# Second block of a two-block layer: scaled queries ahead of the diagonal's mask, the stick mixer's VectorE part a turn later, mixed tiles copied during the last gate tile

## The reference

```python
h = x @ w_in
o_nsa = nsa_mixer(...)             # three attention branches, 6 heads
o_sb = stick_breaking_mixer(...)   # 4 heads, blocks of 128 queries
o_hg = hgrn2_mixer(...)            # 6 heads, gated linear recurrence
o_hg = o_hg * rsqrt(mean(o_hg ** 2) + eps) * hg_norm_w
mixed = concatenate([o_nsa * silu(nsa_z), o_sb * silu(sb_z), o_hg * silu(hg_z)])
x = layer_norm(ALPHA * x + mixed @ w_out, ln_g, ln_b)

# stick breaking, for one block of queries
z = (q @ k.T) * scale
log_rest = where(mask, log_sigmoid(-z), 0)
between = reverse cumulative sum of log_rest, shifted by one
a = where(mask, exp(log_sigmoid(z) + between), 0)
o = a @ v
```

## Time and profile before

| | us |
| --- | --- |
| median of 3 runs | 1101.42 |
| lowest, highest | 1100.38, 1101.49 |
| the profiled execution, its own time | 1101.64 |
| span of that execution | 1099.4 |
| TensorE busy in the span | 1063.4 (97%) |
| VectorE, ScalarE, GpSimd busy | 619.1, 451.4, 27.4 |
| mean granted TensorE clock | 0.994 |

### The profile page before, as it was taken

How to read it: one execution, slowest core, us unless ns; L and a number is a source line. 1 busy time by engine, 2 the same in 40 slices (tenths; PEclk the granted TensorE clock), 3 DMA queues, 4 the chain that set the end, 5 groups by cost and what they waited for, 6 DMA issues and landing times.

```text
span 1099.4 us, 13928 instructions
## 1 busy us (share of the span) xinstructions
PE 1063.4 (97%) x5454; PEld 850.1 (77%) x5454; DVE 619.1 (56%) x1167; ACT 451.4 (41%) x825; POOL 27.4 (2%) x41
## 2 busy tenths in 40 slices
PE   6999999999999999999999999999998899999997
PEld 5877778888879888888888888988776686666575
DVE  5457654445355666532666634445685673566657
ACT  5344333232254444421343434543345456556640
POOL 0000000000011000000000000200000001000000
PEclk9999999999999999999999999999999999999999
DMA  7421123323332832341332233242111123310011
GB/s 264 154 78 58 58 77 96 96 96 96 118 115 74 298 106 89 118 129 55 96 96 96 96 124 125 92 144 80 57 56 49 39 87 98 151 56 27 16 58 77
DMA packets 29103, 107.06 MB, mean 97 GB/s; under 512 B 3226, under 2 KB 3370, under 8 KB 28400
## 3 DMA queue, kind: packets, MB, share of 16 engines
q1 hardware_dynamic: 24288, 84.04, 23.3%
q0 software_dynamic: 4032, 19.96, 5.2%
q10 hardware_dynamic: 720, 2.20, 0.5%
HBM read 101.44 MB, written 7.36 MB: 99 GB/s over the span
## 4 chain that ended last, share of the span: by engine, by line
PE 88%; DVE 6%; ACT 3%; issue 2%; DMA 1%; ACTq 0%; DVEq 0%; SPq 0%
PE ps L671 25%; PE ps L673 24%; PE ps L672 24%; PE ps L1050 2%; PE ps L1084 1%; PE ps L1067 1%; PE ps L945 1%; PE ps L811 1%; DVE wlo L1482 1%; PE ps L784 1%; PE ps L1017 1%; PE ps L796 1%; ACT whi L1149 1%; DMA XT<-xt 1%; PE ps L982 1%
## 5 line engine op out<-in xcount | busy, mean ns | idle before, releaser
L671 PE MATMUL ps<-XH,whi 128*128 128x512 f32 (+1 forms) x864 | 338.8, 392 | 9.9 <-DVE wlo L1499 8.3
L673 PE MATMUL ps<-XH,wlo 128*128 128x512 f32 (+1 forms) x864 | 328.2, 380 | 0.0
L672 PE MATMUL ps<-XL,whi 128*128 128x512 f32 (+1 forms) x864 | 328.0, 380 | 0.0
L1482 DVE TENSOR_TENSOR wlo<-raw,whi 128x1024 fp32r<-128x1024 f32 (+1 forms) x158 | 189.3, 1204 | 182.1 <-ACT whi L1149 182.0
L671 PEld LDWEIGHTS ps<-XH,whi 128*128 128x128 f32 x864 | 163.6, 189 | 50.7 <-issue 18.3
L1149 ACT CAST whi<-raw 128x1024 fp32r<-128x1024 f32 (+1 forms) x158 | 161.2, 1026 | 85.9 <-PE ps L673 57.5
L673 PEld LDWEIGHTS ps<-XH,wlo 128*128 128x128 f32 x864 | 163.4, 189 | 31.4
L672 PEld LDWEIGHTS ps<-XL,whi 128*128 128x128 f32 x864 | 163.8, 190 | 27.7 <-issue 0.5
L671 PE MATMUL ps<-whi,GH 128*128 128x512 f32 x176 | 68.9, 391 | 0.0
L672 PE MATMUL ps<-wlo,GH 128*128 128x512 f32 x176 | 68.6, 389 | 0.0
L673 PE MATMUL ps<-whi,GL 128*128 128x512 f32 x176 | 68.5, 389 | 0.0
(11 more groups left out here) (275 smaller groups left out, 1346.6 us busy)
## 6 DMA issues: line engine op xcount, KB each, us to landing
raw<-wp SPq DMA_DIRECT2D x150, 512.0 KB, 3.5
vec_dram<-row_dram POOLq DMA_DIRECT2D x1, 3072.0 KB, 13.1
H<-x POOLq DMA_DIRECT2D x1, 2048.0 KB, 8.1
x_dram<-H POOLq DMA_DIRECT2D x1, 2048.0 KB, 7.6
A<-w1c POOLq DMA_DIRECT2D x2, 1024.0 KB, 6.6
A<-x_dram POOLq DMA_DIRECT2D x1, 2048.0 KB, 12.7
y<-A SPq DMA_DIRECT2D x8, 256.0 KB, 2.0
raw<-wp SPq DMA_DIRECT2D x4, 402.0 KB, 3.6
```

The costliest lines, as they stand in the source:

```text
L671: self.e.matmul(o, ah, bh, start=start, stop=False)
L672: self.e.matmul(o, ah, bl, start=False, stop=False)
L673: return self.e.matmul(o, al, bh, start=False, stop=stop)
L1482: self.e.tensor_tensor(wlo[BUF[i]][:, 0:w], raw[i % NR][:, 0:w], whi[BUF[i]][:, 0:w].bitcast(F), ALU.subtract).then_inc(sems["lo"], 1)
```

## The change

Nothing is computed otherwise. In `hgrn()` the call of `h_q1` stands ahead of `h_diag`, and `h_prep(p, 0)` stands a turn later, behind `h_off(p, 0)`. In `stick()` VectorE's part of `s_first` becomes a stage of its own, `s_soft`, one turn later, and the diagonal's mask of `s_second` becomes `s_mask`, which runs at the head of the next block's `s_first` (after the last block, a turn later). TensorE's and ScalarE's parts stay in `s_first` and `s_second`. In `gates()` the first three `mix_tile` run in the turns of the last gate tile; a new semaphore `zx` says that this tile's matmuls have read the slices of XH that the copies overwrite; `out2` begins a turn earlier. ScalarE's load of the Exp table moves from behind its copy of the last stick result to ahead of it. `nsk` is merged into `vev`, whose waits count one higher.

```diff
@@ hgrn, stick @@
             en.h_start(p)
             yield
+            en.h_q1(p)
             en.h_diag(p)
-            en.h_q1(p)
-            en.h_prep(p, 0)
             yield
             en.h_off(p, 0)
+            en.h_prep(p, 0)
             en.h_prep(p, 1)
             en.h_mult(p, 0)
...
             for n in range(4):
+                if n:
+                    en.s_mask(p, n - 1)
                 en.s_first(p, n)
                 yield
+                en.s_soft(p, n)
                 yield
                 en.s_second(p, n)
                 yield
+            en.s_mask(p, 3)
             yield
             en.s_pv(p)
@@ gates @@
                 if n >= 4 and part == 1:
                     en.mix_mul(n - 4)
+                if n == 7 and part > 0:
+                    en.mix_tile(part - 1)
                 yield
         en.mix_mul(4)
-        en.mix_tile(0)
-        en.mix_tile(1)
+        en.mix_tile(3)
         yield
-        en.mix_tile(2)
+        en.out2(0, 0, 0)
+        en.mix_tile(4)
         yield
...
@@ Tensor @@
-                self.tile(B2_Z + n, part, 4, 2)
+                f = self.tile(B2_Z + n, part, 4, 2)
+                if n == 7 and part < 3:
+                    f.then_inc(sems["zx"], 1)
@@ Scalar @@
-            def nsa_begin(self):
-                self.e.preload_act_table_set(EXP)
...
             def s_pv(self, p):
+                if p == 1:
+                    self.e.preload_act_table_set(EXP)
                 self.wait_ge("s_av", p + 1)
...
                     self.wait_ge("t_m", n + 1)
-                    self.wait_ge("used", SLOT_WOUT2)
+                    if n // 2 < 3:
+                        self.wait_ge("zx", n // 2 + 1)
+                    else:
+                        self.wait_ge("used", SLOT_WOUT2)
@@ Vector @@
-            def s_first(self, p, n):
+            def s_soft(self, p, n):
...
+
+            def s_mask(self, p, n):
+                kb, at = 3 - n, 4 * p + n
                 for j in range(2):
                     diag = AA[j][kb][:, 0:128]
```

More of the change, by code:

```diff
@@ L83 @@
 sq eps rt rs pg nlo nhi tr xh xl tm res
-qev vev nsk qk tt ex t1 cp av sk skx nrm ft ahi alo
+qev vev qk tt ex t1 cp av sk skx nrm ft ahi alo
 cvc cvp cvy cvt cvz cvh cvl gt bra bm ma mh ml
 vem dm ve lb lbe ua ub sl um gh gl
-fb fc hk sc one kl0 qz hq hv hgt avv src nk nq sq2 sk2 zc zt
+fb fc hk sc one kl0 qz hq hv hgt avv src nk nq sq2 sk2 zc zt zx
 h_d h_x h_e h_dg h_ta h_qk h_k2 h_of h_oc h_p h_pe h_m h_pr h_av h_sq h_rm h_ln h_rs h_ot blk1
@@ L174 @@
     c_move = c_blk = c_mm = c_end = begin_norm = block2_after = idle
-    n_qk = n_scale = n_tr = n_pv = n_out = nsa_begin = s_first = s_second = s_pv = mix_mul = mix_tile = mix_rows = last = out2 = end = idle
+    n_qk = n_scale = n_tr = n_pv = n_out = nsa_begin = s_first = s_soft = s_second = s_mask = s_pv = mix_mul = mix_tile = mix_rows = last = out2 = end = idle
 class Engine(Stages):
@@ L444, in gates @@
                     en.mix_mul(n - 4)
+                if n == 7 and part > 0:
+                    en.mix_tile(part - 1)
                 yield
         en.mix_mul(4)
-        en.mix_tile(0)
-        en.mix_tile(1)
+        en.mix_tile(3)
         yield
-        en.mix_tile(2)
+        en.out2(0, 0, 0)
+        en.mix_tile(4)
         yield
[L452 to L459, removed]
+        en.out2(0, 0, 1)
+        en.mix_tile(5)
+        yield
+        en.out2(0, 1, 0)
+        en.mix_rows(0)
+        yield
+        en.out2(0, 1, 1)
+        en.mix_rows(1)
+        yield
         en.mix_rows(2)
@@ L780, in qk @@
                     self.wait_ge("qev", 5)
-                    self.wait_ge("vev", 1)
+                    self.wait_ge("vev", 2)
                     self.wait_ge("tt", 2 * n + j - 1)
@@ L791, in tr @@
                 self.wait_ge("cp", n)
-                self.wait_ge("vev", 2)
+                self.wait_ge("vev", 3)
                 self.wait_ge("par", 32)
@@ L805, in pv @@
                 self.wait_ge("cp", n + 1)
-                self.wait_ge("vev", 4)
+                self.wait_ge("vev", 5)
                 self.wait_ge("nrm", qb)
@@ L1572, in v @@
                     self.wait_ge("rs", 2)
-                    self.e.tensor_scalar(nsink, RW[:, R_SINK:R_SINK + 8], -1.0, None, ALU.mult).then_inc(sems["nsk"], 1)
+                    self.e.tensor_scalar(nsink, RW[:, R_SINK:R_SINK + 8], -1.0, None, ALU.mult).then_inc(sems["vev"], 1)
                 self.wait_ge(*rows_done(0, t, SLOT_V))
@@ L1583, in soft @@
                     self.wait_ge("qk", 2 * n + j + 1)
-                    self.wait_ge("nsk", 1)
+                    self.wait_ge("vev", 1)
                     self.wait_ge("av", n - 2)
```

1 line of the change is left out of this document (added).

## The result

| | before | after |
| --- | --- | --- |
| median, us | 1101.38 | 1108.82 |
| lowest to highest, four runs each | 1100.38 to 1101.49 | 1107.79 to 1109.06 |
| the profiled execution, its own time | 1101.64 | 1108.73 |
| its span, mean granted clock | 1099.4, 0.994 | 1106.5, 0.991 |

The changed kernel takes 1.0077 times as long as the one before (95% interval 1.0064 to 1.0089): 7.4 us more. 1108.2 was predicted, in a range of 1102.3 to 1113.5.

The account below looks back on a forecast made before the run. TensorE, busy for 97% of the span, was taken as the bound outside a few places. Terms -4.8 + 4.9 + 5.5 + 4.4 - 1.2 - 2.2 = +6.6 over 1101.64 gave 1108.2 us, range 1102.3 to 1113.5.

Parts of the forecast that it names:

- stick (0, 2), clock: Two waits below 2 us replace one of 2.53, so the clock stays up: -3.1 us, bounds 0 and -3.1.
- `h_prod` before (0, 3): Next level's h_prep and h_mult come ahead of VectorE's stick part, so h_prod's 2.17 us wait goes: -2.2.
- stick (1, 1), wait and clock: VectorE's part stands behind c_blk(1, 0), which awaits GpSimd's transfer: +4.9 us wait, +2.2 for the lower clock.
- stick (1, 3), wait and clock: VectorE's part stands behind the weight slot's low part, cast after Gelu's table loads: +5.5 us wait, +2.2 clock.
- nsa's begin: ScalarE's table load goes ahead of TensorE's last stick result into idle time; the 1.18 us wait goes: -1.2.
- tail, waits and clock: Gates' tail: the 1.81 us wait goes (-1.8), its low clock (-1.7), new waits +1.3; together -2.2.
- rival 1: The clock also falls at stick (0, 1) or (0, 2): +3.1, 1111.3 us; chance 0.22.
- The clock behind the two long waits: Lower clock after the waits at stick (1, 1) and (1, 3): 2.2 us each, +4.4; bounds 0 and 6.2.
- One sign of being wrong: The prediction is wrong if TensorE's low stretches are as many as before.
- The second: Rival: the clock stays up through the two long waits, as through 2.17: -4.4, 1103.8 us; chance 0.10.
- the fourth: Rival: neither long wait comes, only the gains: -14.8, 1093.4 us; chance 0.08.
- rival 3: Transfer before c_blk(1, 0) lands in 2.2 us, not 5.6; not slower: -5.6, 1102.6 us; chance 0.10.

Follow-up runs that it names:

- the second of the two transfer runs: Changed kernel with the small transfers, still behind the weight's wait for c_mm, issued ahead of the 1 MB transfer: 1102.80 us.
- the tail's run: Kernel before with the gates' tail and the Exp table load alone changed: 1097.52 us, ratio 0.9970.
- the fastest: Changed kernel with only VectorE's part of stick (0, 3) a turn later, other parts at once, masks right behind the second part: 1088.60 us.

## Why the prediction was right

| step | predicted | after shows |
| --- | --- | --- |
| two waits at `h_off` | -2.4 | -2.4 |
| stick (0, 1) | +1.8 | +1.63 |
| stick (0, 2), wait | -0.8 | -1.07 (2.53 to 1.46) |
| stick (0, 2), clock | -3.1 | -1.4 (3.06 to 1.65) |
| `h_prod` before (0, 3) | -2.2 | -2.17, and +0.5 at the picks |
| first `s_pv` | +1.9 | +1.62 |
| stick (1, 1), wait and clock | +4.9, +2.2 | +4.62, +3.0 |
| stick (1, 3), wait and clock | +5.5, +2.2 | +5.54, +1.64 |
| nsa's begin | -1.2 | -1.18 |
| tail, waits and clock | -0.5, -1.7 | -0.6, -1.7 |
| start of the kernel | none | -1.0 in this execution |
| sum | +6.6 | +7.0 (profiled executions: +7.09) |

The first line of the tail's prediction is its -1.8 and +1.3 together. The waits in the tail, from 960 us on, are after 1.5 + 0.8 + 0.3 + 0.2 = 2.8, before 2.5 + 0.5 + 0.4 = 3.4.

**The waits were right**, each within 0.3 us, since each came from the same question: what does the moved instruction now stand behind, and when is that released? Two runs confirm that the releaser was the right one. With (1, 1) at once -8.0 was measured, where the prediction's terms give -7.1; with (1, 3) at once -8.3, against -7.7. The parts that were to gain did so as well: -6.6 for the queries (-8.0 was expected of that run), -3.7 for the tail with nsa's begin (the terms give -3.4).

**The step that was off is the clock at stick (0, 2).** I took it that the clock stays up because two shorter waits stand in place of one of 2.53, and gave the other case to rival 1. What happened lies in between: the clock fell behind a wait of 1.46, but for some 3.4 us instead of 6.8. The reason I gave, the length of the wait, doesn't decide it. Six other runs have the same two waits of 1.6 and 1.4 to 1.5 here. In one of them (with (1, 1) at once) the clock fell, in five it stayed up, as in this one (the second pair at once):

```profile
848.75 0.91 PE L1031 MATMUL ps<-A,C 128*128 128x384 f32 x2 [1.45 <-DVE A L1929]
```

The first two matmuls take 0.91 us here, at the full clock, and 1.47 in the changed kernel's profile. So this term is a chance and not a value, and -3.1 was the end of its range, not its middle.

The clock behind the two long waits was the same kind of guess at 2.2 each, and measured 3.0 and 1.64. It differs since both low stretches are 6.8 us long, but at (1, 1) TensorE stands idle in 0.8 of it and at (1, 3) in 3.5. These two misses cancel within 0.3.

**The sum is in part luck.** All clock terms together were put at -0.4 (-3.1, +4.4, -1.7) and came to +1.5. That the sum is only 0.4 off is due to the start of the kernel, -1.0 in this execution, and to the waits, which were a little shorter than predicted; without the start the rows give +8.0. The start is chance: the first block is the same in all kernels here, and its wait of 1.25 ended between 30.0 and 32.0 us over their profiles. The medians moved by +7.4.

**One sign of being wrong doesn't fit the forecast.** It says that low stretches as many as before would refute it. Before there were two, and the forecast itself puts two in their place, behind stick (1, 1) and (1, 3). There were three; the one near 850 is what the forecast didn't have, and it is in part rival 1.

**A term that was missing** is the one for the picks. With `h_prod` no longer late, TensorE comes earlier to the next one and waits for its pick (0.97 instead of 0.46): +0.5.

**The rivals.** The second (clock up through the long waits) and the fourth (no long waits) fell with the trace. The third, the early landing, needed the transfer to land within 3.2 us. After the change it was issued at 883.54, VectorE was idle from 885.03 on for 4.29 us, and it landed in 5.7 us, not 2.2. The Trainium skill, SBUF - State Buffer, section SBUF: two separate sides, has GpSimd unable to write its descriptors while VectorE runs an operation on both ports, so that an idle VectorE would let the transfer land early. The two landings go the other way: it was late with VectorE idle for most of it, and early, in the second of the two transfer runs, with VectorE at work for most of it. Whether VectorE's operations there use both ports, no run shows. What shortened the landing, at an issue time 0.5 us apart, was to move the 1 MB transfer from ahead of it to behind it. The Trainium skill, DMA: Bandwidth & Descriptors, section Two DMAs through the same engine are not ordered, says that descriptors start in order within one queue of one DMA engine, and with that the two runs agree. The price of rival 3 was sound, though not its cause: with the landing at 2.2 us the kernel takes 1102.8, where it gave 1102.6.

## What to carry to other kernels

In queues that run in order, a step that is moved to give its engine more slack also takes over the waits of everything it is moved behind: list for each instance what now stands ahead and when that is released. One order for all instances of a loop was the mistake here: of eight blocks two lost some 8 us each by the later turn, two others 3.8 together, and one, (0, 3), gained by 1.9 at most. Without the stick's part the change is 1.1% faster than before; the choice for (0, 3) adds little. The same holds for transfers: a small one that an engine waits for goes ahead of a large one in its queue.

## What was not expected of the hardware

The granted clock after a short wait is not the same from one execution or kernel to the next. After the wait of 2.53 us at stick (0, 2) it fell for 6.8 us in the kernel before and not at all in the tail's run; after that of 2.17 at `h_prod` it stayed up before and fell for 3.4 us in two runs. In the tail the wait of 0.78 us, which all kernels with the new tail have, was followed by the lower clock in two (with (1, 1) at once, and with the weight behind) and by the full one in the others. The one of (1, 1) at once, where the eight matmuls take 1.91 us instead of 1.11:

```profile
1028.87 1.91 PE L1081 MATMUL ps<-C,A 128*128 128x128 f32 x8 [0.78 <-DVE A L1907]
```

```profile
1029.00:1032.40 3.40, 3.40 (x12) 1.89 (x12) 3.36 (x10) 2.49 (x7) 0.00 (x0) 0.50 0.00 0
```

Between 740 us and the last matmuls every low stretch of these profiles was about 3.4 or 6.8 us long, that is 1.7 or up to 3.4 us lost. That this spreads the runs of one kernel is likely but not shown, since only one execution of each was profiled. Three versions had no low stretch there in their profile: their runs stay within 0.6 us (the fastest), 1.5 (the second pair at once) and 2.2 (queries and tail). The tail's ten runs spread over 6.2, and the mean granted clock doesn't order them strictly: two took 1098.5 us, at 0.996 and at 0.993. Why one wait of 1.46 us is followed by it and the same wait in another kernel is not, these runs don't settle.
